# The last two experts' outputs stacked on 128 partitions, and tile 1's second choice moved to TensorE

## The reference

```python
def _hier_moe(x, rg, rgb, re, reb, wg, wu, wd):
    t = x.reshape(B * T, D)
    pg = jax.nn.softmax(t @ rg + rgb)                     # 4 groups
    p_top, g_idx = lax.top_k(pg, 1)
    le = (t @ re + reb).reshape(-1, N_GROUPS, EXPERTS_PER_GROUP)
    le_g = jnp.take_along_axis(le, g_idx[:, :, None], axis=1)[:, 0]
    q, e_idx = lax.top_k(jax.nn.softmax(le_g), TOP_K_INNER)   # 2 of 8
    ...
    h = silu(einsum('nd,edf->nef', t, wg)) * einsum('nd,edf->nef', t, wu)
    y = einsum('nef,efd->nd', h * comb[:, :, None], wd)
x = x + _hier_moe(_rmsnorm(x, norm2), ...)
y_prompt, y_sample = _rmsnorm(hp, final_norm), _rmsnorm(hs, final_norm)
```

## Time and profile before

| what | value |
| --- | --- |
| runs | 774.0, 773.29, 771.27 us |
| profiled execution | 774.38 us, its span 772.5 us |
| PE busy | 741.7 us (96%) |
| DVE, ACT, POOL busy | 447.3, 240.4, 61.2 us |
| chain that ended last | PE 88%, DMA 4%, DVE 2%, ACT 2% |
| HBM read, written | 154.43 MB, 15.73 MB |

### The profile page before, as it was taken

One profiled execution on the slowest core, in us unless ns is written; L12 is line 12 of the kernel. 1 busy time (PEld: TensorE's weight loads), 2 busy tenths in 40 slices (PEclk: granted clock), 3 DMA queues, 4 the chain that ended last, 5 costly groups with the idle time before them and its releaser, 6 DMA issues.

```text
span 772.5 us, 18138 instructions
## 1 busy us (share of the span) xinstructions
PE 741.7 (96%) x7029; PEld 458.5 (59%) x7029; DVE 447.3 (58%) x1194; ACT 240.4 (31%) x593; POOL 61.2 (8%) x71
## 2 busy tenths in 40 slices
PE   5999999999999999999999999999899999999896
PEld 4566666666666666666676666454455555555442
DVE  4365677777777777777767875616533332223225
ACT  4224343353352452552453452322100001000014
POOL 3000000400000000000000000000132312131110
PEclk9999999999999999999999999999999999999999
DMA  9443142771170160260161373398999999999995
GB/s 246 121 112 109 29 132 78 138 197 37 27 193 14 29 194 10 62 171 15 54 165 27 115 307 144 100 395 307 402 420 419 420 418 418 420 419 420 418 383 204
DMA packets 117286, 160.06 MB, mean 207 GB/s; under 512 B 27718, under 2 KB 92032, under 8 KB 110824
## 3 DMA queue, kind: packets, MB, share of 16 engines
q1 hardware_dynamic: 100692, 147.57, 53.1%
q0 software_dynamic: 5760, 7.80, 3.9%
q10 hardware_dynamic: 10789, 4.06, 2.0%
HBM read 154.43 MB, written 15.73 MB: 220 GB/s over the span
## 4 chain that ended last, share of the span: by engine, by line
PE 88%; DMA 4%; DVE 2%; ACT 2%; issue 1%; SPq 1%; ACTq 1%; POOLq 0%; DVEq 0%
PE bank L820 24%; PE bank L1270 12%; PE bank L1277 6%; PE bank L1002 5%; PE bank L826 5%; PE bank L1082 4%; PE bank L1140 4%; DMA scratch<-in_exp_up 3%; PE bank L792 2%; PE bank L1309 2%; PE bank L944 2%; PE bank L935 2%; PE bank L1034 1%; PE bank L854 1%; PE bank L1109 1%
## 5 line engine op out<-in xcount | busy, mean ns | idle before, releaser
L820 PE MATMUL bank<-xnT,wall 128*128 128x320 f32 x656 | 194.7, 441 | 0.0
L820 PEld LDWEIGHTS bank<-xnT,wall 128*128 128x128 f32 x656 | 118.6, 190 | 45.1 <-issue 2.6
L708 POOL DMA_INDIRECT merged<-xn2d,gidx x15 | 15.5, 1036 | 513.1 <-DVE gidx L2259 403.9
L2303 DVE COPY vecs<-bank 128x512 f32<-128x512 f32 x32 | 22.1, 691 | 58.1 <-PE bank L1277 29.5
L2308 DVE TENSOR_TENSOR scratch<-bank,n 128x512 f32<-128x512 f32 x30 | 20.5, 687 | 49.9 <-PE bank L1270 45.7
L1002 PE MATMUL bank<-xnT,wall 128*128 128x320 f32 x128 | 47.9, 456 | 0.3
L1702 ACT ACTIVATE vecs<-bank 128x128 f32<-128x128 f32 x32 | 8.9, 277 | 117.6 <-PE bank L1270 117.6
L1270 PE MATMUL bank<-scratch 128*64 128x256 f32 x320 | 38.4, 395 | 3.4 <-DMA scratch<-in_exp_up 3.0
L1270 PE MATMUL bank<-vecs,scratch 128*64 128x256 f32 x352 | 40.6, 382 | 0.6 <-DVE scratch L2233 0.6
L1469 ACT ACTIVATE shared<-bank 128x256 f32<-128x256 f32 x32 | 12.3, 385 | 73.5 <-PE bank L820 66.8
L1082 PE MATMUL bank<-xnT,wall 128*128 128x320 f32 x112 | 33.1, 439 | 0.7
(11 more groups left out here) (447 smaller groups left out, 1359.1 us busy)
## 6 DMA issues: line engine op xcount, KB each, us to landing
wall<-in_w_in SPq DMA_DIRECT2D x58, 512.0 KB, 5.4
scratch<-in_exp_gate SPq DMA_DIRECT2D x10, 1024.0 KB, 14.0
scratch<-in_exp_up SPq DMA_DIRECT2D x10, 1024.0 KB, 16.1
vecs<-in_exp_gate SPq DMA_DIRECT2D x10, 1024.0 KB, 9.6
vecs<-in_exp_up SPq DMA_DIRECT2D x10, 1024.0 KB, 11.9
scratch<-in_exp_down SPq DMA_DIRECT2D x6, 1024.0 KB, 14.0
shared<-in_exp_gate SPq DMA_DIRECT2D x10, 512.0 KB, 14.8
shared<-in_exp_up SPq DMA_DIRECT2D x10, 512.0 KB, 16.1
```

The costliest lines, as they stand in the source:

```text
L708: pool.indirect_dma_start(rows, None, xn2d, bass.IndirectOffsetOnAxis(ap=e, axis=0), bounds_check=N - 1, oob_is_err=False).then_inc(S(sem) ...
L820: q = mm(tpbank(L, name), wbuf[name][:, k, :], xnT[:, k, :], start=(k == 0), stop=(k == KC - 1))
L2303: CP(ye[:, e % 2, :], bank[6 + e % 2][:]).then_inc(S("ye"), 1)
```

## The change

The outputs of experts 30 and 31 are laid out the other way: each expert has one half of the partitions and the two column halves go to banks 6 and 7 (`dn_last`). DVE copies bank 6 and ACT bank 7 when both experts are done. One one-hot matrix a tile, with both experts on its 128 rows, then serves both column halves, so `hots` is half as large as `dup`. The transposed activations go to columns 256 to 383 of banks 2 and 3, and bank 4 becomes free for tile 1's sum; its two residual products move behind experts 18 and 20. Tile 1's second choice is no longer multiplied and added by DVE; PE adds it with a diagonal matrix `gate1`, as for tile 2. On ACT the two scalings by the first gate stand ahead of the table load.

```diff
...
-        dup = late[:, 640:1408].rearrange("p (t e c) -> p t e c", t=3, e=ON_CHIP)
+        slotT = [late[:, 0:128], late[:, 128:256], late[:, 256:320]]
+        gate1 = late[:, 320:448]
+        hots = late[:, 640:1024].rearrange("p (t e s) -> p t e s", t=3, e=ON_CHIP)
-        fb = [bank[j] for j in (0, 1, 2, 5, 4)]
+        fb = [bank[j] for j in (0, 1, 4, 5, 2)]
...
             def turn_h(e):
-                tr(bank[4][:, 0:128], hh, ident).then_inc(S("hT_ps"), 1)
+                tr(bank[2 + e % 2][:, 256:384], hh, ident).then_inc(S("hT_ps"), 1)
+            def dn_last(x):
+                e = NE - ON_CHIP + x
+                pe.wait_ge(S("hT"), e + 1)
+                landed(e, "d")
+                if x == 0:
+                    pe.wait_ge(S("ye"), NE - ON_CHIP)
+                for j in range(2):
+                    for d in range(2):
+                        q = mm(bank[6 + d][at64(x), :], hT[:, 64 * j:64 * j + 64], down(buf(e), j, d), start=(j == 0), stop=(j == 1))
+                q.then_inc(S("dn"), 1)
...
             def hot_out(t):
-                for x in range(ON_CHIP):
-                    pe.wait_ge(S("ye"), NE - ON_CHIP + 1 + x)
-                    for d in range(2):
-                        b = fb[2 * t + d][:] if t < 2 else fb[4][at64(d), :]
-                        q = mm(b, slotT[t][at64(d), x, :], ye[at64(d), x, :], start=False, ...)
-                if t < 2:
+                pe.wait_ge(S("ye"), NE)
+                for d in range(2):
+                    b = fb[2 * t + d][:] if t < 2 else fb[4][at64(d), :]
+                    q = mm(b, slotT[t], ye[:, d, :], start=False, stop=(t == 0), skip_group_check=True)
+                if t == 0:
                     q.then_inc(S("fin_ps"), 1)
...
+                if e == 18:
+                    before_experts(2)
+                if e == 20:
+                    pe.wait_ge(S("late"), 4)
+                    before_experts(3)
             dn(NE - 3)
-            for j in (0, 1, 3):
+            for j in range(2):
                 before_experts(j)
             up(NE - 2)
             up_last(0)
             turn_h(NE - 2)
-            before_experts(2)
             up_last(1)
-            dn(NE - 2)
+            dn_last(0)
             turn_h(NE - 1)
-            dn(NE - 1)
-            hot_out(0)
-            hot_out(1)
+            dn_last(1)
             before_experts(4)
-            hot_out(2)
+            for t in range(3):
+                hot_out(t)
...
+            pe.wait_ge(S("ya11"), 16)
+            for d in range(2):
+                last = mm(fb[2 + d][:], gate1, ya[1][:, 1, 512 * d:512 * d + 512], start=False, stop=True, skip_group_check=True)
+            last.then_inc(S("fin_ps"), 1)
```

On ACT and DVE:

```diff
+            act.wait_ge(S("dn"), NE)
+            act.wait_ge(S("y_out1"), 8 * (NE - ON_CHIP))
+            A(ye[:, 1, :], bank[7][:], ACT.Copy).then_inc(S("ye"), 1)
...
-            A(warm[:], misc[:, 3:4], ACT.Sqrt)
             for t in range(2):
                 act.wait_ge(S(f"ya0{t}"), 16)
                 A(ya[0][:, t, :], ya[0][:, t, :], ACT.Identity, scale=r1[:, t, 8:9]).then_inc(S("ya_g"), 1)
+            A(warm[:], misc[:, 3:4], ACT.Sqrt)
...
-            outputs(NE - 1)
+            dve.wait_ge(S("dn"), NE)
+            dve.wait_ge(S("y_out0"), 8 * (NE - ON_CHIP))
+            CP(ye[:, 0, :], bank[6][:]).then_inc(S("ye"), 1)
...
                 dve.wait_ge(S("ya_g"), t + 1)
-                dve.wait_ge(S(f"ya1{t}"), 16)
-                go(STT(ya[1][:, t, :], ya[1][:, t, :], r1[:, t, 9:10], ya[0][:, t, :], MUL, ADD))
+                y = ya[0]
+                if t == 0:
+                    y = ya[1]
+                    dve.wait_ge(S("ya10"), 16)
+                    go(STT(y[:, t, :], y[:, t, :], r1[:, t, 9:10], ya[0][:, t, :], MUL, ADD))
                 dve.wait_ge(S("fin_ps"), t + 1)
```

More of the change, by code:

```diff
@@ L401, in hawk_rwkv7_moe @@
         late = consts[:, CONST["blk"][0]:CONST["m1"][1]]
-        slotT = [late[:, 256 * t:256 * t + 256].rearrange("p (e c) -> p e c", e=ON_CHIP) for t in range(2)]
-        slotT.append(late[:, 512:640].rearrange("p (e c) -> p e c", e=ON_CHIP))
-        dup = late[:, 640:1408].rearrange("p (t e c) -> p t e c", t=3, e=ON_CHIP)
+        slotT = [late[:, 0:128], late[:, 128:256], late[:, 256:320]]
+        gate1 = late[:, 320:448]
+        hots = late[:, 640:1024].rearrange("p (t e s) -> p t e s", t=3, e=ON_CHIP)
         fnb = consts[:, CONST["blk"][0] + 640:CONST["blk"][0] + 640 + D]
         gate2 = [vrows, vT]
-        fb = [bank[j] for j in (0, 1, 2, 5, 4)]
+        fb = [bank[j] for j in (0, 1, 4, 5, 2)]
         sl2, ge, ge2 = (sb(n, [P, 3 * ON_CHIP]).rearrange("p (t e) -> p t e", t=3) for n in ("sl2", "ge", "ge2"))
@@ L1330, in slot_rows @@
                     for t in range(2):
-                        for x in range(ON_CHIP):
-                            q = tr(bank[5][:, 256 * t + 128 * x:256 * t + 128 * x + 128], dup[:, t, x, :], ident)
+                        q = tr(bank[5][:, 128 * t:128 * t + 128], hots[:, t].rearrange("p e s -> p (e s)"), ident)
                 else:
                     pe.wait_ge(S("late"), 1)
-                    for x in range(ON_CHIP):
-                        q = tr(bank[5][:, 64 * x:64 * x + 64], dup[0:64, 2, x, :], ident[0:64, 0:64])
+                    q = tr(bank[5][:, 0:64], hots[0:64, 2].rearrange("p e s -> p (e s)"), ident[0:64, 0:64])
                 q.then_inc(S("late_ps"), 1)
@@ L1353, in hot_out @@
             def hot_out(t):
-                for x in range(ON_CHIP):
-                    pe.wait_ge(S("ye"), NE - ON_CHIP + 1 + x)
-                    for d in range(2):
-                        b = fb[2 * t + d][:] if t < 2 else fb[4][at64(d), :]
-                        q = mm(b, slotT[t][at64(d), x, :], ye[at64(d), x, :], start=False, stop=(x == 1 and t < 2), skip_group_check=True)
-                if t < 2:
+                pe.wait_ge(S("ye"), NE)
[3 more added lines that the diff above has]
+                if t == 0:
                     q.then_inc(S("fin_ps"), 1)
@@ L1385, in _ @@
                     final_gains(1)
+                if e == 18:
[3 more added lines that the diff above has]
+                    before_experts(3)
             dn(NE - 3)
-            pe.wait_ge(S("late"), 4)
             pe.wait_ge(S("gT"), NE)
-            for j in (0, 1, 3):
+            for j in range(2):
                 before_experts(j)
@@ L1705, in _ @@
                 act.wait_ge(S("hT_ps"), e + 1)
-                A(hT, bank[4][:, 0:128], ACT.Copy).then_inc(S("hT"), 1)
+                A(hT, bank[2 + e % 2][:, 256:384], ACT.Copy).then_inc(S("hT"), 1)
                 if e in (14, 16):
@@ L2279, in slots @@
                     go(TS(gate2[q][:], ident, r1[:, 2, 8 + q:9 + q], None, MUL))
+                go(TS(gate1, ident, r1[:, 1, 9:10], None, MUL))
                 for t in range(3):
-                    go(TT(dup[:, t].rearrange("p e (d s) -> p e d s", d=2), sl2[:, t, :, None, None].broadcast_to([P, ON_CHIP, 2, CAP]),
-                          C("j64")[:, None, None, :].broadcast_to([P, ON_CHIP, 2, CAP]), EQ))
+                    go(TT(hots[:, t], sl2[:, t, :, None].broadcast_to([P, ON_CHIP, CAP]),
+                          C("j64")[:, None, :].broadcast_to([P, ON_CHIP, CAP]), EQ))
                 ch.wait()
                 for t in range(3):
-                    q = TT(dup[:, t], dup[:, t], ge[:, t, :, None].broadcast_to([P, ON_CHIP, 2 * CAP]), MUL)
+                    q = TT(hots[:, t], hots[:, t], ge[:, t, :, None].broadcast_to([P, ON_CHIP, CAP]), MUL)
                     if t < 2:
@@ L2293, in slot_columns @@
                 if part == 0:
-                    CP(late[:, 0:512], bank[5][:]).then_inc(S("late"), 1)
+                    CP(late[:, 0:256], bank[5][:, 0:256]).then_inc(S("late"), 1)
                 else:
-                    CP(late[:, 512:640], bank[5][:, 0:128]).then_inc(S("late"), 1)
+                    CP(late[:, 256:320], bank[5][:, 0:64]).then_inc(S("late"), 1)
             def outputs(e):
@@ L2324, in _ @@
                     gained(e // 2 + 1, 1, bank[1])
-                if e and e != NE - 2:
+                if 0 < e < NE - 2:
                     outputs(e - 1)
@@ L2359, in gathered @@
                     c = slice(512 * d, 512 * d + 512)
-                    q = TT(x1[:, t, c], ya[1][:, t, c], fb[2 * t + d][:], ADD)
+                    q = TT(x1[:, t, c], y[:, t, c], fb[2 * t + d][:], ADD)
                     if d == 0:
```

## The result

The changed kernel takes 776.69 us (median of 5 runs, 776.13 to 777.89); the kernel before takes 772.3 us (median of 5). The ratio is 1.0061, 95% interval 1.0047 to 1.0074: slower by 3.6 to 5.7 us, beyond what a run of this kernel can tell from no change. The forecast was 776.9.

A forecast was written before the change was run, and what follows sets the result against it. PE bounds the last 30 us unless weights are missing. Its terms, -1.72 + 3.44 - 1.05 + 1.72 = +2.39, become +3.6 at the end through tile 1's later DVE and ACT work: 773.29 + 3.6 = 776.9 us, range 773.4 to 779.0.

The forecast's parts named there:

- Stacked down products: Down products of experts 30 and 31 (`dn_last`): each group 3.44 us instead of 1.72, together +3.44 us.
- Rival A: Stacked down products still run two at a time, taking 3.44 us off: 773.6 us, not slower; chance 0.12.
- One-hot products: One-hot products with tile 2's residual product at the end: 5.5 us instead of 6.55, -1.05 us, both bank copies hidden.
- What is late next: DVE's tile 1 additions wait for the new gate products; tile 2's square starts behind tile 1's root: +3.6 us at the end.
- the three signs: A `dn_last` under 2.5 us, PE waiting for weights at expert 31, or ACT's tile 1 work done before PE's last product.
- Moved residuals: Tile 1's two residual products leave PE's stretch around experts 30 and 31 for places behind experts 18 and 20: -1.72 us, uncut.
- Tile 1's second choice: Two more products on PE, +1.72 us; DVE's 1.28 us multiply-add falls away but lay beside PE.
- Covers: Waits at experts 27 and 28 hide the added loop work; 2.3 us of room covers ACT's gates-first order: 0 each.
- rival C: Later PE in the loop delays the loads, the 1.3 us shift coming on top: 778.2 us; chance 0.08.
- Rival B: Added work shortens the wait at expert 28, the clock stays up, PE is 1.7 us earlier: 775.2 us; chance 0.13.

## Why the prediction was right, point by point

**Stacked down products: right.** +3.44 was forecast for two groups; they take 3.62 + 3.65 against 1.72 + 1.94, +3.6. Counted from 753.75, where the first group of before starts on PE's timeline, that group took 1.89, and the difference is 3.44. Undone, the last part is 2.3 us shorter, where 2.4 (3.44 less the 1.05 of the one-hot products) was forecast. The cause is shown by the alternating order: 3.65 us for sixteen instructions instead of eight. Rival A falls. The rule of the Trainium skill that was weighed there (page "TensorE: Matmul & The Clock Gate", section "Why this matters for your kernels": narrow products run side by side when their outputs lie in distinct column groups) agrees with these rows: 3.65 us for sixteen with neighbours in different halves, 3.62 and 3.65 for eight in one.

**One-hot products: right.** 5.5 us forecast for the residual and the products, 5.5 measured; half as many instructions, full width, no gain for tiles 0 and 1. Both copies of the outputs end within the residual's time (759.56 and 759.47, the residual at 759.88).

**What is late next: right in the profile.** The additions of tile 1 start at 766.34 behind the new products, tile 2's square behind tile 1's root. From the new products' end to the last scaling's end it is 5.25 us, as forecast (5.3). None of the three signs by which the prediction would be wrong came.

**Moved residuals: the step that failed.** "So the gain is not cut" looked at the weights of expert 31 and not at those of expert 30, whose margin is smaller. Their last DMA issue before:

```profile
L594 SPq DMA_DIRECT2D wkv<-in_exp_down x2: 1062/1231/1400, 737.1 to 738.6; - x2
...
DMA to landing us min/median/max: 12.0/13.0/14.1
```

The issue at 738.6 lands after 14.1 us, at 752.7; PE came to these weights at 753.75, so only about 1.05 us lay there. The term was 1.72; alone the part wins 1.1 to 1.3 us in the profiles (part of which may be the clock, as said above), and in the change 1.25, with PE waiting 0.33 us for those weights (the gap at 750.55). In before and in the change expert 28 took 5.36 us, so these two compare like with like. For the last part the forecast was 3.6 + 1.72 = 5.3, and 5.30 was measured: the whole 0.45 by which the tail is longer than forecast (4.05 against 3.6) comes from this term.

**Tile 1's second choice: right in this kernel's sum, but not a price that can be added.** I counted 1.72 on PE and 1.1 behind it, and said that DVE's multiply-add "lay beside PE". It did before; in the stacked kernel it does not. With the residuals moved, the last part in the profiles is

| last part, us | outputs in halves | outputs stacked |
| --- | --- | --- |
| second choice on DVE | 15.4 | 19.3 |
| second choice on PE | 18.3 | 20.6 |

(the first without the gates first; with them, and one residual product in a gap, it is 15.3). The gate products alone cost 2.9, near the 2.8 that I counted, but for the other kernel; stacking alone costs 3.9; both cost 5.2 and not 6.8, since each makes tile 1 late by itself. In the kernel with halves the price of 2.9 looks like that of a place in the queue: tile 1's additions wait until 764.75 (762.82 + 1.93 on the chain there) for products that stand behind tile 2's one-hot products, while tile 1's own end at 759.89 (756.25 + 3.64) and its rows have landed at about 760.1 (750.8 + 9.3). No run puts the products there, so this is argued and not shown.

**Covers: right.** The work added in the loop is hidden, and 1.7 us more would be too (rival C falls). The order of gates and table load is worth 0 here. Rival B does not come to pass: where expert 28 took 3.67 us, PE waited for weights afterwards and the tail stayed 46.6 to 46.8.

The measured difference of the medians is 776.69 - 772.3 = 4.4 us, and the interval of the ratio gives 3.6 to 5.7; the traces give 4.05. The forecast of 3.6 stands at the low end, short by the term above. The absolute time came out closer than the difference, 776.9 against 776.69, and that is luck: the difference was 0.8 us too small, and the median of before is 1 us lower over five runs (772.3) than over the three (773.29) to which I added.

What stays open: how much of the 1.2 us that the moved residuals win in two profiles comes from them, and whether it is there in the times. The intervals of both runs reach to 1.

## What to carry to other kernels

Half-array products cost nothing extra here while neighbours in the queue use different halves (eight in 1.72 to 1.94 us); an order that keeps a group on one half doubles it (3.62 to 3.65), so count the halves of successive instructions and not the instructions. Before moving work from an engine beside the path onto the engine on the path, look at who is waiting for whom in the new kernel: here the work on DVE came onto the path only by the other half of the change, and its new place in PE's queue stood behind tile 2's one-hot products. Where a stage runs just behind its loads, an earlier start of PE is worth at most the smallest landing margin of all the loads in the stage, and not its own length.

## What the runs showed of the hardware

After a wait of PE of about 2 us its clock was lower in some executions and not in others. Expert 28's products took 5.36 us, at a mean granted clock of 0.68 of 2.4 GHz, after waits of 2.06 (before) and 1.92 (the change), and 3.67, at 1.00, after 2.04 in the moved residuals' profile and 2.07 in the one with the table load first. A gap of that size can't be priced from one profile; in the kernels with the change the 1.7 us never reached the end.
